# Where the second half of a shared expert's products runs: between the first experts, or ahead of them

## The chip, the cores and the metric

The kernel runs on one core of one Trainium2 chip. The metric is device time in microseconds (us) of one execution. The kernel before took 1657.83 us, the median of three runs from 1657.65 to 1658.01 us. All numbers of the inside of the kernel are from one further execution, which the hardware profiler recorded.

## The reference, cut to what matters

A decoder trunk with two layers over 272 tokens (16 learned ones and 256 of the input) of width 1024, all in float32. Each layer has a token mixer (RWKV-7 in layer 0, sliding-window attention in layer 1) and then a mixture of experts, which is where the change lies:

```
def swiglu(x, wg, wu, wd):
    return (jax.nn.silu(x @ wg) * (x @ wu)) @ wd

def moe_ffn(x2d, router, bias, w_gate, w_up, w_down, sh_gate, sh_up, sh_down):
    ...  # each token picks 8 of 64 experts; the tokens of an expert are gathered
    y = swiglu(x2d[tok], w_gate[e], w_up[e], w_down[e])     # for each expert
    ...
    return swiglu(x2d, sh_gate, sh_up, sh_down) + routed    # and one shared expert for all tokens
```

Each expert has a gate and an up matrix of 1024 x 256 and a down matrix of 256 x 1024: 1 MB each, 3 MB an expert, 192 MB a layer. The shared expert has the same shapes and is applied to all 272 tokens.

## The kernel before, in words

The program has one instruction stream for each engine. They meet at semaphores, and within one engine the order is that of the program.

**The stream of expert weights.** SyncE (SP) issues all expert weights, each as one transfer of 1 MB, in the order gate and up of expert e, then down of expert e-1 (`sp_experts`, which calls `sp_load`, issue in line 844). On chip there is room for four experts. So the first four experts' weights are fetched while the token mixer still runs. Gate and up of expert 4 may be issued only when the gate and up product of expert 0 is done (semaphore `L.gu`), and so on with a distance of four; a down matrix waits for the down product four experts earlier (`L.down`).

**One expert on TensorE** (`pe_expert`), in this order: the gate and up product (`mm_gate_up`, line 781, 16 matmuls, 32 passes in the trace, since each float32 matmul shows as two); the turning of the next expert's gathered token rows (`pe_turn_x`, line 769); the pick of the indices of the expert three ahead (`pe_pick`, line 762); the turning of this expert's gate and up results (line 788); and the down product of the expert before (`mm_down`, line 799). VectorE copies the turned rows out of PSUM before the next gate and up product can start (line 774).

**The gathers.** GpSimd fetches the token rows of an expert by an indirect transfer (line 818) when VectorE has turned the picked values into indices (`take_index`, lines 812 to 814), and writes scaled results back by another (line 823).

**The shared expert.** Its 256 hidden columns are done in two halves of 128, as each half's result fills a PSUM bank. `mm_shared` (line 1006) issues for each of the eight slices of the width one matmul of 128 x 128 weights with 272 token columns. The first half of gate and of up (`sg0`, `su0`) is issued during the routing, ahead of the experts. The second half (`sg1`, `su1`) uses the same two banks, so `sg1` may start when ScalarE has read `sg0` (semaphore step `sg0` of `moe_act`), and `su1` when VectorE has multiplied the first half (step `sm0` of `moe_dve`, line 1050). In the kernel before it stands between the experts: four matmuls of `sg1` after expert 0 and four after expert 1, four of `su1` after expert 2 and four after expert 3. ScalarE applies silu to `sg1` after its part of expert 2, and after its part of expert 4 it waits for `su1` and issues the load of the shared down matrix (1 MB, on its own queue).

**Ahead of the first expert** (`pe_experts`), TensorE issues one product without use, the picks for experts 0, 1 and 2, each of which waits for VectorE, then four products without use (`keep_busy`, line 998: 512 columns each, 8 passes in the trace; the result goes to a bank that is overwritten), and then turns the rows of expert 0.

`SETS` = 4 is the number of experts held, `E` = 64 the number of experts.

Of the kernel before, what the change touches and what calls it, by code (L numbers as in the profile page):

```python
# [35 lines left out]
KC = D // P  # L36
# [84 lines left out]
def hybrid_trunk(nc, I, out):  # L121
    with ExitStack() as ctx:
# [3 lines left out]
        def sem(name):  # L126
            return ctx.enter_context(nc.semaphore(name))
# [125 lines left out]
        def ln_steps(t, halves=True):  # L253
# [29 lines left out]
                  for l in range(2)]  # L283
        moe_act = [Steps(sem(f"route_act{l}"), [(f"hT{t}", 1) for t in H_ORDER[l]] + [("sig", 1), ("sc", 1), ("sg0", 1), ("sg1", 1)]) for l in range(2)]
        moe_dve = [Steps(sem(f"route_dve{l}"),
                         [(f"{n}{t}", 1) for n, t in zip(("hT", "row", "hT", "row", "row"), ROW_ORDER[l])]
                         + [("choice", 1), ("top2", 24), ("gs", 1), ("rank", 5), ("hide", 1), ("mask", 1),
                            ("top8", 3), ("taken", 3), ("sel", 1), ("g0", 1), ("gsum", 1), ("g1", 1), ("g2", 1),
                            ("kr", 1), ("dest", 3), ("posm", 1), ("max", 1), ("maxi", 1), ("sm0", 1), ("sm1", 1),
                            ("sd", 6)]) for l in range(2)]  # L290
# [425 lines left out]
        def num(e, times=1, add=0, per=1):  # L716

            i, k = e
            v = times * (k // per) + add
            return v if isinstance(i, int) else i * (UNROLL * times // per) + v  # L720

        def wait(eng, s, value):

            if not isinstance(value, int) or value > 0:
                eng.wait_ge(s, value)

        def early(e, k):

            return isinstance(e[0], int) and e[1] == k

        def plus(e, k):
            return (e[0], e[1] + k)
# [6 lines left out]
        def e_slots(e):  # L739

            s0 = 3 * (e[1] % SETS)
            return s0, s0 + 1, s0 + 2
# [34 lines left out]
        def mm_gate_up(dst, s):  # L777

            for k in range(KC):
                for j in range(2):  # L780
                    mm = nc.tensor.matmul(dst[SLOTS * j:SLOTS * j + SLOTS, 0:FF], xgT[:, k, :],  # L781
                                          slot_of(s + j)[:, FF * k:FF * k + FF], start=(k == 0), stop=(k == KC - 1))
            return mm

        def mm_turn(dst):

            for j in range(2):
                mm = nc.tensor.transpose(dst[:, P * j:P * j + P], guc[:, P * j:P * j + P], ident[:, :])  # L788
            return mm
# [5 lines left out]
        def mm_down(dst, s, hid):  # L795

            for j in range(2):
                for half in range(2):
                    mm = nc.tensor.matmul(dst[SLOTS * half:SLOTS * half + SLOTS, :], hid[:, j, :],  # L799
                                          slot_of(s)[:, D * j + 512 * half:D * j + 512 * half + 512],  # L800
                                          start=(j == 0), stop=(j == 1))
            return mm
# [43 lines left out]
        def pe_pick(pe, L, e):  # L846

            pe.wait_ge(L.onehot, num(e, 1, L.base + 1))
            wait(pe, L.index, num(e, 1, L.base))
            mm_pick(ps[:, bV, :], hot[e[1] % 2], column(values, e, 3)).then_inc(L.values, 1)  # L850

        def pe_turn_x(pe, L, l, e):
            pe.wait_ge(L.gathered[e[1] % 4], num(e, 16, 4 * L.base + 16, per=4))
            wait(pe, L.xt_copied, num(e, 1, L.base))
            mm_turn_x(ps[:, bU, :], xs[e[1] % 4]).then_inc(L.xt, 1)

        def pe_expert(pe, L, l, e, this=True):
            after, three_after, prev = ahead(e, 1), ahead(e, 3), e_before(e)
            if this:
                s0, s1, _ = e_slots(e)  # L860
                pe.wait_ge(L.xt_copied, num(e, 1, L.base + 1))
                pe.wait_ge(slot_loaded[s0], num(e, 16, L.slot_base[s0] + 16, per=SETS))
                pe.wait_ge(slot_loaded[s1], num(e, 16, L.slot_base[s1] + 16, per=SETS))
                wait(pe, L.gu_copied, num(e, 1, L.base))
                mm_gate_up(ps[:, bG, :], s0).then_inc(L.gu, 1)
            if this and after:
                pe_turn_x(pe, L, l, plus(e, 1))
            if this and three_after:
                pe_pick(pe, L, plus(e, 3))
            if this:  # L870
                copied, hidden = num(e, 1, L.base + 1), num(e, 1, L.base)
                if not isinstance(copied, int):
                    pe.reg_add(copied_count, copied_count, 1)
                    pe.reg_add(hidden_count, hidden_count, 1)
                    copied, hidden = copied_count, hidden_count
                pe.wait_ge(*moe_dve[l].at("choice"))
                pe.wait_ge(L.gu_copied, copied)
                wait(pe, L.hid, hidden)
                mm_turn(ps[:, bR, :]).then_inc(L.turned, 1)
            if prev:  # L880
                q = plus(e, -1)
                s2 = e_slots(q)[2]
                pe.wait_ge(L.hid, num(q, 1, L.base + 1))
                if early(q, 0):
                    pe.wait_ge(*moe_dve[l].at("maxi"))
                pe.wait_ge(slot_loaded[s2], num(q, 16, L.slot_base[s2] + 16, per=SETS))
                wait(pe, L.y_a, num(q, 1, L.base - 1))
                wait(pe, L.y_v, num(q, 1, L.base - 1))
                mm_down(ps[:, bY[q[1] % 2], :], s2, hidT[q[1] % 2]).then_inc(L.down, 1)
# [78 lines left out]
        def over_experts(eng, body):  # L968

            for k in range(HEAD):  # L970
                body((0, k))
            with eng.Fori(0, (E - HEAD - TAIL) // UNROLL) as i:
                for j in range(UNROLL):
                    body((i, HEAD + j))
            for k in range(E - TAIL, E):
                body((0, k))

        def ahead(e, k):

            return not isinstance(e[0], int) or e[1] + k < E  # L980

        def e_before(e):
            return not isinstance(e[0], int) or e[1] >= 1
# [9 lines left out]
        SPARE_BANK = (7, 2)  # L993

        def keep_busy(bank, n):

            for _ in range(n):
                nc.tensor.matmul(ps[:, bank, :], ident[:, :], headrow[:, 0:512], start=True, stop=True)  # L998

        def mm_shared(pe, l, name, ks):  # L1000

            which, half = name[1], int(name[2])
            j = "gu".index(which)
            for k in ks:
                w = shared_w[j][:, FF * k:FF * k + FF].rearrange("p (m j) -> p j m", j=2)
                m = nc.tensor.matmul(ps[:, bS[j], 0:T], w[:, half, :], mhT[:, k, :], start=(k == 0), stop=(k == KC - 1))  # L1006
                if k == KC - 1:
                    m.then_inc(*moe_pe[l].step(name))

        def pe_experts(pe, L, l):  # L1010
            pe.reg_mov(copied_count, num((0, HEAD - 1), 1, L.base + 1))
            pe.reg_mov(hidden_count, num((0, HEAD - 1), 1, L.base))
            keep_busy(SPARE_BANK[1], 1)
            pe_pick(pe, L, (0, 0))
            pe_pick(pe, L, (0, 1))
            pe_pick(pe, L, (0, 2))
            keep_busy(SPARE_BANK[1], 4)
            pe_turn_x(pe, L, l, (0, 0))

            def body(e):  # L1020
                pe_expert(pe, L, l, e)
                if early(e, 0):
                    pe.wait_ge(*moe_act[l].at("sg0"))
                if early(e, 2):
                    pe.wait_ge(*moe_dve[l].at("sm0"))
                if isinstance(e[0], int) and e[1] < 4:
                    mm_shared(pe, l, ("sg1", "su1")[e[1] // 2], range(KC // 2 * (e[1] % 2), KC // 2 * (e[1] % 2) + KC // 2))
            over_experts(pe, body)
            pe_expert(pe, L, l, (0, E), this=False)

        def act_silu(act, l, half):
# [357 lines left out]
        def _(pe):  # L1389
# [373 lines left out]
            def moe(l, prev_dve):  # L1763
# [36 lines left out]
                m.then_inc(*st.step("pos"))  # L1800
                set_main(l)
                pe_experts(pe, main, l)
                pe.wait_ge(*moe_dve[l].at("sm1"))
                pe.wait_ge(shared_loaded[2], 16 * (l + 1))
# [1002 lines left out]
```

## Time and profile before

| what | value |
|---|---|
| runs, median (lowest to highest) | 1657.83 us (1657.65 to 1658.01) |
| span of the profiled execution, first to last instruction | 1659.9 us, 33659 instructions |
| mean granted TensorE clock | 0.968 |
| TensorE busy | 1469.7 us (89%) |
| VectorE, ScalarE, GpSimd busy | 619.0, 318.7, 331.5 us |
| DMA moved | 508.21 MB, mean 306 GB/s; 456.49 MB of it on SP's queue |

The profile states no time of the profiled execution but its span, which is 2.07 us (0.12%) above the median of the runs. Times inside the trace count from the first instruction. The experts of layer 0 run from about 388 to 902 us, those of layer 1 from about 1102 to 1617 us. PE is TensorE's matmuls, SPq the issue of transfers by SP, DVE VectorE, ACT ScalarE, POOL GpSimd. "PEclk" is the granted TensorE clock as a share of its upper level, 2.4 GHz, so that 0.50 is the lower level, 1.2 GHz. "DMA share" is the mean busy share of the 16 DMA engines; it can read a little over 1.

### The profile page before, as it was taken

How to read it: one execution, taken by the hardware profiler on the slowest of the kernel's cores; microseconds unless marked ns; L12 is line 12 of the kernel's file. 1: busy time of each engine (PE TensorE's matmuls, PEld its weight loads, DVE VectorE, ACT ScalarE, POOL GpSimd, SP SyncE). 2: the span in 40 equal slices, each digit the busy share in tenths (PEclk: the TensorE clock that was granted, in tenths of full speed). 3: DMA queues.
4: the chain of work that ended last, by engine and by line, in shares of the span. 5: the costliest groups of instructions: out<-in, count | busy, mean ns of one | idle time of the engine just before them, and what ended most of it. 6: DMA issues, size and time to landing. Idle time of an engine off the chain costs nothing.

```text
span 1659.9 us, 33659 instructions
## 1 busy us (share of the span) xinstructions
PE 1469.7 (89%) x12824; PEld 952.7 (57%) x12824; DVE 619.0 (37%) x1580; ACT 318.7 (19%) x743; POOL 331.5 (20%) x412
## 2 busy tenths in 40 slices
PE   6989988899998888888888698999998888888886
PEld 4776877656665555555554267466655555555542
DVE  5362352673333333333332704543333333333327
ACT  1521332110111111111111015111111111111110
POOL 6012000021222222222221210122222222222210
PEclk9999988899999999999999799999999999999998
DMA  6330002349999999999997961299999999999986
GB/s 198 124 113 1 4 4 80 105 175 370 403 414 415 416 415 415 415 416 415 415 416 312 366 184 52 94 376 396 414 415 416 416 415 415 416 415 416 416 339 246
DMA packets 139862, 508.21 MB, mean 306 GB/s; under 512 B 29273, under 2 KB 58273, under 8 KB 104188
## 3 DMA queue, kind: packets, MB, share of 16 engines
q1 hardware_dynamic: 103312, 456.49, 68.9%
q0 software_dynamic: 22288, 41.89, 7.0%
q10 hardware_dynamic: 14172, 8.54, 1.8%
q8 instruction: 67, 1.10, 0.3%
q14 instruction: 23, 0.19, 0.0%
HBM read 501.38 MB, written 36.90 MB: 324 GB/s over the span
## 4 chain that ended last, share of the span: by engine, by line
PE 44%; SPq 23%; DMA 22%; DVE 6%; issue 3%; ACT 1%; ACTq 0%; DVEq 0%; POOL 0%; POOLq 0%
SPq L844 23%; DMA arena<-in_moe_w_up 21%; PE ps L781 9%; PE ps L1423 6%; PE ps L799 3%; PE ps L1553 3%; PE ps L1006 2%; PE ps L1865 2%; PE ps L1967 2%; PE ps L762 1%; PE ps L769 1%; PE ps L1748 1%; DMA arena<-routed 1%; PE ps L1849 1%; PE ps L998 1%
## 5 line engine op out<-in xcount | busy, mean ns | idle before, releaser
L781 PE MATMUL ps<-arena 128*64 128x256 f32 x2048 | 234.5, 381 | 57.2 <-DMA arena<-in_moe_w_up 57.2
L781 PE MATMUL ps<-ring,arena 128*64 128x256 f32 x2048 | 234.6, 381 | 51.8 <-DMA ring<-in_moe_w_up 38.5
L774 DVE COPY arena<-ps 128x512 f32<-128x512 f32 x128 | 88.6, 692 | 514.1 <-PE ps L769 514.1
L781 PEld LDWEIGHTS ps<-arena 128*64 128x64 f32 x2048 | 163.4, 137 | 151.5 <-issue 106.4
L818 POOL DMA_INDIRECT arena<-hrows,arena x128 | 129.7, 1013 | 586.0 <-DVE arena L814 572.0
L781 PEld LDWEIGHTS ps<-ring,arena 128*64 128x64 f32 x2048 | 154.5, 137 | 154.0 <-issue 79.0
L823 POOL DMA_INDIRECT routed<-arena x128 | 118.2, 924 | 240.2 <-DVE arena L942 175.8
L942 DVE TENSOR_SCALAR arena<-ps,arena 64x512 f32<-64x512 f32 x128 | 95.1, 743 | 162.1 <-PE ps L799 162.1
L896 ACT COPY arena<-ps 128x256 f32<-128x256 f32 x128 | 47.6, 372 | 537.0 <-PE ps L781 537.0
L906 ACT ACTIVATE arena<-ps,arena 64x512 f32<-64x512 f32 x128 | 87.5, 683 | 206.1 <-PE ps L799 206.1
L799 PE MATMUL ps<-ring,arena 128*64 128x512 f32 x512 | 124.0, 605 | 0.0
L799 PE MATMUL ps<-arena 128*64 128x512 f32 x512 | 123.5, 604 | 0.0
L762 PEld LDWEIGHTS ps<-arena 128*128 128x128 f32 (+1 forms) x768 | 105.6, 190 | 6.1 <-issue 2.3
L762 PE MATMUL ps<-arena 128*128 (+2 forms) x768 | 105.8, 242 | 2.1 <-DVE arena L814 1.6
L769 PE MATMUL ps<-ident,arena 128*128 128x128 f32 x512 | 83.8, 286 | 0.0
L769 PEld LDWEIGHTS ps<-ident,arena 128*128 128x128 f32 x512 | 53.7, 140 | 49.7 <-issue 49.7
L1423 PE MATMUL ps<-arena,ring 128*128 128x272 f32 x256 | 63.9, 415 | 8.8 <-DVE arena L2342 4.4
L806 DVE SCALAR_TENSOR_TENSOR arena<-arena 128x384 f32<-128x384 f32 x128 | 69.1, 541 | 0.1
L900 ACT ACTIVATE arena<-ps 128x128 f32<-128x128 f32 x128 | 35.5, 277 | 152.4 <-PE ps L788 152.4
L1423 PEld LDWEIGHTS ps<-arena,ring 128*128 128x128 f32 x256 | 51.7, 203 | 20.8 <-DVE arena L2292 4.8
L799 PEld LDWEIGHTS ps<-arena 128*64 128x64 f32 x512 | 31.2, 136 | 48.1 <-issue 48.1
L799 PEld LDWEIGHTS ps<-ring,arena 128*64 128x64 f32 x512 | 31.0, 136 | 47.3 <-issue 47.3
(375 smaller groups left out, 1595.4 us busy)
## 6 DMA issues: line engine op xcount, KB each, us to landing
ring<-in_moe_w_gate SPq DMA_DIRECT2D x64, 1024.0 KB
ring<-in_moe_w_up SPq DMA_DIRECT2D x64, 1024.0 KB
ring<-in_moe_w_down SPq DMA_DIRECT2D x64, 1024.0 KB
arena<-in_moe_w_gate SPq DMA_DIRECT2D x64, 1024.0 KB
arena<-in_moe_w_up SPq DMA_DIRECT2D x64, 1024.0 KB
arena<-in_moe_w_down SPq DMA_DIRECT2D x64, 1024.0 KB
arena<-routed SPq DMA_DIRECT2D x16, 1024.0 KB, 14.3
ring<-in_attn_w_qkv SPq DMA_DIRECT2D x6, 1024.0 KB
```

Of the source, the lines that this page charges most:

```text
L762: mm = nc.tensor.matmul(dst[:, 0:3], hot[0:n, t, :], vals[0:n, t, :], start=(t == 0), stop=(t == NT - 1))
L769: mm = nc.tensor.transpose(dst[:, P * j:P * j + P], rows[:, P * j:P * j + P], ident[:, :])
L774: return nc.vector.tensor_copy(xgT.rearrange("p (r j) m -> p j r m", r=2), ps[:, bU, :].rearrange("p (j r m) -> p j r m", j=4, r=2))
L781: mm = nc.tensor.matmul(dst[SLOTS * j:SLOTS * j + SLOTS, 0:FF], xgT[:, k, :], slot_of(s + j)[:, FF * k:FF * k + FF], start=(k == 0), stop= ...
L799: mm = nc.tensor.matmul(dst[SLOTS * half:SLOTS * half + SLOTS, :], hid[:, j, :], slot_of(s)[:, D * j + 512 * half:D * j + 512 * half + 512 ...
L806: return nc.vector.scalar_tensor_tensor(out=hot, in0=iota_s[:, order, :].unsqueeze(1).to_broadcast([P, NT, 2 * SLOTS]), scalar=float(first ...
L818: return nc.gpsimd.indirect_dma_start(out=dst, out_offset=None, in_=hrows_d[l], in_offset=bass.IndirectOffsetOnAxis(ap=index, axis=0), bou ...
L823: return nc.gpsimd.indirect_dma_start(out=routed[l], out_offset=bass.IndirectOffsetOnAxis(ap=index, axis=0), in_=src, in_offset=None, boun ...
L844: sp.dma_start(slot_view(s), src).then_inc(slot_loaded[s], 16)
L906: nc.scalar.activation(ysc[q[1] % 4][:, 512:1024], ps[SLOTS:P, bY[q[1] % 2], :], ACT.Copy, scale=gate_s[q[1] % 8][SLOTS:P]).then_inc(L.y_a, 1)
L942: nc.vector.tensor_scalar(ysc[q[1] % 4][:, 0:512], ps[0:SLOTS, bY[q[1] % 2], :], gate_s[q[1] % 8][0:SLOTS], None, ALU.mult).then_inc(L.y_v, 1)
L1423: m = mm_(b[:, 0:T], slot3(s)[:, k, P * (c % 2):P * (c % 2) + P], xm[MIXBUF[mix]][:, k, :], start=(k == 0), stop=(k == KC - 1))
```

## The change

The four products without use that stand between the picks and the turning of expert 0's rows are taken out. In their place stands the whole second half of the shared expert's gate and up products, 16 matmuls (32 passes) of 272 columns, with the two waits on `sg0` and `sm0`. The four pieces between experts 0 to 3 are gone, so that each expert runs straight after the one before. The other engines' streams are as they were.

```
             pe_pick(pe, L, (0, 2))
-            keep_busy(SPARE_BANK[1], 4)
+            pe.wait_ge(*moe_act[l].at("sg0"))
+            mm_shared(pe, l, "sg1", range(KC))
+            pe.wait_ge(*moe_dve[l].at("sm0"))
+            mm_shared(pe, l, "su1", range(KC))
             pe_turn_x(pe, L, l, (0, 0))
-
-            def body(e):
-                pe_expert(pe, L, l, e)
-                if early(e, 0):
-                    pe.wait_ge(*moe_act[l].at("sg0"))
-                if early(e, 2):
-                    pe.wait_ge(*moe_dve[l].at("sm0"))
-                if isinstance(e[0], int) and e[1] < 4:
-                    mm_shared(pe, l, ("sg1", "su1")[e[1] // 2], range(KC // 2 * (e[1] % 2), KC // 2 * (e[1] % 2) + KC // 2))
-            over_experts(pe, body)
+            over_experts(pe, lambda e: pe_expert(pe, L, l, e))
             pe_expert(pe, L, l, (0, E), this=False)
```

The function that both versions call:

```
        def mm_shared(pe, l, name, ks):
            which, half = name[1], int(name[2])
            j = "gu".index(which)
            for k in ks:
                w = shared_w[j][:, FF * k:FF * k + FF].rearrange("p (m j) -> p j m", j=2)
                m = nc.tensor.matmul(ps[:, bS[j], 0:T], w[:, half, :], mhT[:, k, :], start=(k == 0), stop=(k == KC - 1))
                if k == KC - 1:
                    m.then_inc(*moe_pe[l].step(name))
```

## Rows read from the trace of the kernel before

**Rows 1.** The page: TensorE's busy time, and the DMA share in 40 slices.

```profile
PE 1469.7 (89%) x12824; PEld 952.7 (57%) x12824; DVE 619.0 (37%) x1580; ACT 318.7 (19%) x743; POOL 331.5 (20%) x412
...
DMA  6330002349999999999997961299999999999986
```

**Rows 2.** The chain that ended last, in order of time (start, us, what).

```profile
497.28 25.20 DMA arena<-in_moe_w_up
```

**Rows 3.** Stages: window, busy us per engine (instructions), PEclk, DMA share, GB/s.

```profile
500.00:600.00 100.00, 87.62 (x648) 54.59 (x644) 30.59 (x86) 16.08 (x37) 24.13 (x25) 1.00 1.02 415
...
1214.00:1314.00 100.00, 87.08 (x640) 53.94 (x638) 30.50 (x86) 16.00 (x37) 24.10 (x25) 1.00 1.02 415
```

**Rows 4.** Stages of two us about the end of expert 0's product, layer 0.

```profile
390.00:392.00 2.00, 2.00 (x22) 1.17 (x18) 0.00 (x0) 0.00 (x0) 0.00 (x0) 1.00 0.07 29
392.00:394.00 2.00, 2.00 (x16) 1.80 (x15) 0.99 (x4) 0.52 (x2) 0.00 (x0) 1.00 0.52 70
```

**Rows 5.** Timeline of SP: gate loads of experts 4 and 5 in layer 0.

```profile
392.25 0.33 SPq L844 DMA_DIRECT2D ring<-in_moe_w_gate  x1
...
399.46 0.35 SPq L844 DMA_DIRECT2D ring<-in_moe_w_gate  x1
```

**Rows 6.** Timeline of TensorE: start, us, line, operands, count.

```profile
26.57 10.77 PE L1423 MATMUL ps<-arena,ring 128*128 128x272 f32 x35 [4.35 <-DVE arena L2292]
...
366.40 6.69 PE L1006 MATMUL ps<-arena 128*128 128x272 f32 x28
...
380.68 6.63 PE L998 MATMUL ps<-headrow,ident 128*128 128x512 f32 x8
387.15 0.60 PE L769 MATMUL ps<-ident,arena 128*128 128x128 f32 x4
...
393.65 2.01 PE L1006 MATMUL ps<-arena 128*128 128x272 f32 x8
...
402.66 2.11 PE L1006 MATMUL ps<-arena 128*128 128x272 f32 x8
...
1095.13 6.10 PE L998 MATMUL ps<-headrow,ident 128*128 128x512 f32 x8
1101.07 0.60 PE L769 MATMUL ps<-ident,arena 128*128 128x128 f32 x4
```

**Rows 7.** Stages: the granted clock ahead of the first expert, layers 0 and 1.

```profile
379.80:386.60 6.80, 6.80 (x12) 3.36 (x12) 0.99 (x6) 0.00 (x0) 2.31 (x3) 0.50 1.02 417
...
1093.20:1100.00 6.80, 6.30 (x12) 3.61 (x13) 1.33 (x9) 0.00 (x0) 3.05 (x3) 0.50 1.03 421
```

**Rows 8.** Stages of line 1423 alone: PE, PEld, then PEclk, DMA share, GB/s.

```profile
31.00:31.60 0.60, 0.60 (x3) 0.48 (x2) 0.50 0.36 143
31.60:33.00 1.40, 1.40 (x7) 1.13 (x7) 0.99 0.01 3
```

**Rows 9.** Line 1006: duration of one pass (ns, min/median/max), first and last start.

```profile
L1006 PE MATMUL ps<-arena x128: 392/392/506, 365.0 to 1136.5; 128*128 128x272 f32 x128
```

**Rows 10.** Line 1050 on VectorE (end of the first half), and the gathers' landing.

```profile
381.37 0.44 DVE L1050 TENSOR_TENSOR arena<-arena,ps 128x272 f32<-128x272 f32 x1
...
DMA to landing us min/median/max: 6.2/6.7/7.7
```

**Rows 11.** Stages of ten us after the restart of the weight stream, layers 0 and 1.

```profile
400.00:410.00 10.00, 10.00 (x68) 6.27 (x69) 3.37 (x11) 1.34 (x3) 1.95 (x2) 1.00 1.01 383
410.00:420.00 10.00, 10.00 (x66) 5.90 (x68) 2.78 (x8) 2.01 (x5) 1.98 (x3) 1.00 1.01 395
420.00:430.00 10.00, 10.00 (x68) 5.90 (x66) 2.49 (x7) 1.34 (x3) 2.81 (x3) 1.00 1.01 388
...
1114.00:1124.00 10.00, 10.00 (x67) 6.27 (x69) 3.29 (x11) 1.40 (x4) 1.95 (x2) 1.00 1.04 417
1124.00:1134.00 10.00, 10.00 (x66) 5.90 (x66) 2.78 (x8) 1.95 (x5) 2.08 (x3) 1.00 0.99 372
1134.00:1144.00 10.00, 10.00 (x68) 5.88 (x65) 2.49 (x7) 1.34 (x3) 2.82 (x3) 1.00 0.99 380
```

## The prediction

> **What bounds the kernel now.** I read the page first, then the chain in order of time, then the experts' stage in windows. The page says TensorE is busy 89% of the span, but its DMA line stands at 9 in two long stretches [rows 1]; these are the experts of the two layers, and they need windows of their own. There the chain is a trap. It follows TensorE through the experts to 497 us and only there steps over to a weight transfer [rows 2], as if TensorE set the time until then. But a chain that follows a transfer goes back to its issue, and does not see that the transfer stood in a queue: this one took 25.20 us for 1 MB, while the windows show 415 GB/s, at which 1.05e6 bytes need 2.5 us. So some ten transfers stood ahead of it. The windows settle it: over a hundred us of each layer the DMA share is 1.02 at 415 GB/s, while TensorE is busy 87 of 100 us [rows 3]. The weight stream is the bound of this stage, and it ends a fixed time after its last idle moment: bytes left over rate. What counts for the change is therefore when the stream is not at its full rate.
>
> There are two such places. First, before expert 4's weights. The four sets on chip are full at about 390 us; SP may go on when expert 0's gate and up product is done, and issues at 392.25 [rows 5]. In between the stream falls to 29 and then 70 GB/s [rows 4]. Second, after that restart. For 30 us it runs at 383, 395 and 388 GB/s in layer 0 and at 417, 372 and 380 in layer 1, in place of 415 [rows 11]. Here TensorE frees sets hardly faster than they are fetched: an expert with a piece of the shared product is 9.1 us (from 393.65 to 402.66, piece to piece [rows 6]), and 3.15 MB of weights at 415 GB/s are 7.6 us, without the gathers. The queue runs nearly dry before each issue.
>
> **The change, part by part.** *The stretch ahead of expert 0.* Before, 8 passes without use start at 380.68 and the turning of expert 0's rows at 387.15; in layer 1 at 1095.13 and 1101.07 [rows 6]. The clock stands at 0.50, its lower level of 1.2 GHz, from 379.8 to 386.6 and from 1093.2 to 1100.0 [rows 7], after the short picks that wait for VectorE. In place come 32 passes of 272 columns. At the upper level one costs 0.233 us: 28 take 6.69 us, less 0.39 for the last one's duration, over 27 steps [rows 6, 9]. At the lower level I take twice that, 0.467 us. That can be tested on line 1423, which has the same shape and begins at the lower level: it starts at 26.57, the clock rises at 31.6 [rows 8], so 5.03 / 0.467 = 10.8 passes, and the remaining 10.77 - 0.39 - 5.03 = 5.35 us hold 22.9 more; with the last one 34.7 against 35 counted [rows 6]. The same rows show that a stream of this shape is followed by a rise of the clock as the products without use are.
>
> With the rise where it is now, layer 0 does (386.6 - 380.68) / 0.467 = 12.7 passes slowly and 19.3 x 0.233 = 4.5 us of the rest, to 391.1; the turning starts 3.95 us later than 387.15. Layer 1: (1100.0 - 1095.13) / 0.467 = 10.4, then 21.6 x 0.233 = 5.0, to 1105.0, which is 3.95 us later than 1101.07. Both layers: **+7.9 us**. Nothing hides this: the rows' gather, the weights of expert 0 and VectorE's copy are done or follow the turning as they do now. Expert 0's product, and with it SP's issue at 392.25, moves by the whole of it, and the stream is idle in that time.
>
> *The waits.* `sg0` is read by ScalarE during the routing. `sm0` comes from line 1050, which ends at 381.8 [rows 10]; `su1` is reached after 16 slow passes at the earliest, 380.68 + 16 x 0.467 = 388.1. Behind the wait would stand the turning and all experts, but it is met 6.3 us early, so its cost is 0, and 0 again in layer 1, where VectorE's order is the same. The bounds of a wait that passes at once are 0 and one pass, 0.5 us in both layers together; I take 0.
>
> *The pieces between experts.* Eight passes leave each of experts 0 to 3: 2.01 us of the first, 2.11 of a later one [rows 6], 8.3 us by these rows, 32 x 0.233 = 7.5 by the passes. TensorE then reaches expert 4 about 4 us earlier in each layer, in spite of the start. But TensorE is not the bound, so this is worth only what the stream was slowed by: the shortfall from 415 GB/s. Over ten us each it is 0.77, 0.48 and 0.65 us in layer 0 and -0.05, 1.04 and 0.84 in layer 1, as 10 x (415 - rate) / 415 [rows 11]; together 3.7 us. How much comes back no row shows, so it lies between 0 and 3.7; a gain over 3.7 would need a rate above 415, which no long window has. I take the last two of each three, **-3.0 us**: the first stretch still has only the 3 MB that expert 0's product releases, and the next set follows when expert 1's product is done (7.2 us later now, 399.46 [rows 5], about 5.3 then). After that sets come free every 7.0 us (9.1 less a piece of 2.1), quicker than the 7.6 us of a fetch, so the queue fills.
>
> The Trainium skill, page "DMA: Bandwidth & Descriptors", section "Rules for kernel authors", says that a transfer's fixed setup cost overlaps when it is issued early. By that rule a deeper queue would hide all of the shortfall, and the sum would be 7.9 - 3.7 = +4.2 us; the trace agrees so far as the full rate stands where the queue is deep, but no run here shows the queue deepened at this place.
>
> *What else moves.* The picks inside the experts, and the gathers that POOL issues from them, come 3.95 us later for expert 3 and then relatively earlier. A gather lands within 6.2 to 7.7 us [rows 10] and is needed two experts after its pick, some 14 us after without the pieces; a gather that is late would cost TensorE a few tenths, and the queue covers that. The load of the shared down matrix on ScalarE's queue waits for `su1`, which is done long before; it stays behind ScalarE's part of expert 4, with the same 1 MB. VectorE's and ScalarE's instructions are unchanged and wait for less.
>
> **Sum:** 7.9 - 3.0 = +4.9 us on the span of 1659.9 us, so 1664.8. The runs shown have a median 2.07 us below that span; the same difference on it gives 1657.83 + 4.9 = **1662.7 us**, +0.3%. What this measurement can tell from no change is about 0.2%, 3.3 us.
>
> **The rivals.**
>
> *Nothing of the shortfall comes back* (the dips are the gathers' or the memory's doing, not the queue's): +7.9, 1665.7 us. For it: the DMA share is already 0.99 to 1.04 in the slow stretches [rows 11]. Against it: gathers run all through the stage, and later it holds 415.
>
> *TensorE is the bound up to 497 us after all*, as the chain has it [rows 2]. Then the pieces' 8 us less the start's 3.95 count in full, 4.05 a layer, and the time is 1657.83 - 8.1 = 1649.7 us, faster. It would need spare DMA between 394 and 497, of which rows 11 show less than 2 us a layer. Chance small.
>
> *The clock rises late.* If the shared passes did not bring the clock up before they end, 32 x 0.467 = 14.9 us would end at 395.6 and 1110.0, 8.5 and 9.0 us later than now; with -3.0 that is +14.5, 1672.3 us. Line 1423 speaks against it [rows 8].
>
> *More comes back than the shortfall in those stretches*, because the stream's rate from 394 on is raised a little everywhere: at +3 or below this reads as no change, about 1660. Or the idle time at the start proves shorter than the shift, with the same result: the four sets would have to be full later than 390, which row 390 to 392 speaks against [rows 4].
>
> **How the numbers follow.** The forecast's own case, from all of the shortfall back to most of it lost (+3.8 to +6.5): 0.60. Nothing back: 0.14. Late clock: 0.03. Little or no net change: 0.14. TensorE the bound: 0.09. Slower by over 0.2% takes the first three, 0.77, less 0.02 for a forecast that falls just below the line: 0.75; within 0.2%: 0.16; faster: 0.09. The range leaves out the fast case, the late clock and a little of the third and reaches from 1660.2 to 1666.0, from +2.4 to just over the case with nothing back.
>
> **What would show it.** In the profile after: the turning of expert 0 at about 391.1 and 1105.0, with 32 passes of line 1006 ahead of it and the clock at 0.50 until about 386.6 and 1100.0; SP's first issue at about 396.2; an idle stretch of the stream from 390 to about 397; the ten us windows from 406 on at 410 to 416 GB/s; experts 0 to 3 at 7 us each. The prediction is wrong if the first issue comes less than 3 us later, if the stream shows gaps after it as before, or if the last product of layer 0 comes earlier than now although the first issue came later.

## The result, and the profile after

The changed kernel takes 1663.85 us, the median of 20 runs (1657.60 to 1675.65), against 1657.92 us for the kernel before (20 runs, 1652.50 to 1670.36): a ratio of 1.0038, 95% interval 1.0022 to 1.0055. Timed once more beside before (e7 below) it is 1.0021, 1.0001 to 1.0041. So it is slower, by some 0.2 to 0.4%; 1662.7 us was forecast.

The profiled execution seems to say the opposite: its span is 1656.8 us, shorter than the 1659.9 us of before. It was one of the shorter executions of the changed kernel (1658.51 us, fourth lowest of the 20). The page, to be held against [rows 1]:

```profile
span 1656.8 us, 33627 instructions
...
PE 1455.1 (88%) x12808; PEld 951.3 (57%) x12808; DVE 618.3 (37%) x1580; ACT 318.7 (19%) x743; POOL 330.3 (20%) x412
...
DMA  6420002358999999999998961389999999999986
```

The contradiction is solved by counting each layer's experts from their own beginning. TensorE's timeline of the changed kernel (start, us, line, operands, count): the first pick of each layer, in layer 0 the second pick with the idle time ahead of it, the 32 passes, the turning, and the gate and up product of expert 63.

```profile
371.77 0.92 PE L762 MATMUL ps<-arena 128*128 128x3 f32 x6
373.21 0.89 PE L762 MATMUL ps<-arena 128*128 128x3 f32 x6 [0.53 <-DVE arena L814]
...
375.83 10.49 PE L1006 MATMUL ps<-arena 128*128 128x272 f32 x32
386.15 0.60 PE L769 MATMUL ps<-ident,arena 128*128 128x128 f32 x4
...
891.18 3.67 PE L781 MATMUL ps<-arena 128*64 128x256 f32 x32 [1.37 <-DMA arena<-in_moe_w_up]
...
1086.28 0.92 PE L762 MATMUL ps<-arena 128*128 128x3 f32 x6
...
1090.76 9.72 PE L1006 MATMUL ps<-arena 128*128 128x272 f32 x32
1100.32 0.60 PE L769 MATMUL ps<-ident,arena 128*128 128x128 f32 x4
...
1605.39 3.68 PE L781 MATMUL ps<-arena 128*64 128x256 f32 x32 [1.33 <-DMA arena<-in_moe_w_up]
```

SP's timeline of the changed kernel, which answers to [rows 5]: the gate loads of experts 4 and 5 in layer 0, and of expert 4 in layer 1.

```profile
391.25 0.33 SPq L844 DMA_DIRECT2D ring<-in_moe_w_gate  x1
...
396.62 0.35 SPq L844 DMA_DIRECT2D ring<-in_moe_w_gate  x1
...
1105.42 0.33 SPq L844 DMA_DIRECT2D ring<-in_moe_w_gate  x1
```

And the rows of the kernel before that are needed for the same count: first pick and last gate and up product of each layer on TensorE,

```profile
376.65 0.92 PE L762 MATMUL ps<-arena 128*128 128x3 f32 x6
...
894.38 3.67 PE L781 MATMUL ps<-arena 128*64 128x256 f32 x32 [1.36 <-DMA arena<-in_moe_w_up]
...
1090.84 0.92 PE L762 MATMUL ps<-arena 128*128 128x3 f32 x6
...
1608.58 3.67 PE L781 MATMUL ps<-arena 128*64 128x256 f32 x32 [1.39 <-DMA arena<-in_moe_w_up]
```

and SP's first issue in layer 1 (the one in layer 0 is in [rows 5]):

```profile
1106.17 0.33 SPq L844 DMA_DIRECT2D ring<-in_moe_w_gate  x1
```

The differences of these starts, with those of the experiments' profiles, worked out in the same way (us; "start" is from the first pick to the first issue for expert 4, "stream" from there to the start of expert 63's product; layer 0 / layer 1):

| kernel | start | stream | both together |
|---|---|---|---|
| before | 15.60 / 15.33 | 502.13 / 502.41 | 517.73 / 517.74 |
| before, second profile (e8) | 15.59 / 15.29 | 502.12 / 502.00 | 517.71 / 517.29 |
| changed | 19.48 / 19.14 | 499.93 / 499.97 | 519.41 / 519.11 |
| changed, second profile (e7) | 19.34 / 19.08 | 500.22 / 500.12 | 519.56 / 519.20 |
| e1 pieces left out | 15.20 / 15.38 | 500.23 / 500.03 | 515.43 / 515.41 |
| e2 start later still | 22.91 / 22.54 | 500.23 / 499.98 | 523.14 / 522.52 |
| e3 shared down load early | 19.48 / 19.30 | 497.76 / 497.62 | 517.24 / 516.92 |
| e4 begun between the picks | 15.07 / 15.07 | 500.15 / 499.97 | 515.22 / 515.04 |
| e5 = e4 and e3 | 15.07 / 15.07 | 497.65 / 498.17 | 512.72 / 513.24 |
| e6 half of it ahead | 15.56 / 15.48 | 500.14 / 500.39 | 515.70 / 515.87 |

The change makes the start 3.88 and 3.81 us later and the stream 2.20 and 2.44 us shorter: +1.68 and +1.37, together +3.05 us. With the two second profiles it is +1.85 and +1.91, +3.76 us. The stages of one kernel repeat within 0.5 us. What hides them in a single span is the time before the first pick, which is 4.9 us shorter in this profile of the changed kernel, and the time between the layers, 1.4 us shorter; e7 and e8 tell of both.

The chain reads as before ([rows 2]): TensorE first, then a transfer that took 25 us because it queued.

```profile
494.02 25.14 DMA arena<-in_moe_w_up
```

The windows of the changed kernel (busy us per engine, PEclk, DMA share, GB/s) answer to [rows 7], [rows 4], [rows 11] and [rows 3], in that order:

```profile
374.90:381.60 6.70, 6.70 (x18) 5.27 (x18) 0.99 (x6) 0.00 (x0) 2.33 (x3) 0.50 1.03 421
...
388.00:390.00 2.00, 2.00 (x22) 1.33 (x20) 0.00 (x0) 0.00 (x0) 0.00 (x0) 1.00 0.00 0
390.00:392.00 2.00, 2.00 (x20) 1.40 (x16) 0.16 (x1) 0.37 (x1) 0.00 (x0) 1.00 0.00 0
392.00:394.00 2.00, 2.00 (x18) 1.44 (x19) 1.59 (x6) 0.28 (x1) 0.34 (x1) 1.00 0.86 242
394.00:400.00 6.00, 6.00 (x48) 3.56 (x46) 1.33 (x6) 0.70 (x3) 1.79 (x2) 1.00 1.00 414
400.00:410.00 10.00, 10.00 (x84) 6.16 (x80) 3.65 (x9) 2.36 (x5) 2.90 (x3) 1.00 1.02 413
410.00:420.00 10.00, 10.00 (x74) 6.09 (x72) 3.77 (x12) 1.98 (x5) 2.25 (x3) 1.00 1.03 417
...
500.00:600.00 100.00, 86.73 (x631) 53.64 (x632) 30.32 (x86) 16.27 (x37) 23.20 (x25) 1.00 1.02 415
```

Here one sees both sides of the change: four whole us at 0 GB/s while TensorE is at work, and then the full rate from the first window on, where layer 0 of before had 383 to 395. The six us ahead of [rows 11], in the kernel before:

```profile
394.00:400.00 6.00, 6.00 (x48) 4.08 (x46) 0.87 (x3) 0.50 (x2) 1.14 (x1) 1.00 0.97 399
```

### The profile page after: what moved, and what is told of

Its sections match the earlier page's. It is cut to its first block, busy times and chain, and to the rows that moved or that the text cites. A ratio compares the mean times of both kernels' runs of the same rounds, so it can differ in the third digit from the quotient of the medians.

```text
span 1656.8 us, 33627 instructions
## 1 busy us (share of the span) xinstructions
PE 1455.1 (88%) x12808; PEld 951.3 (57%) x12808; DVE 618.3 (37%) x1580; ACT 318.7 (19%) x743; POOL 330.3 (20%) x412
## 4 chain that ended last, share of the span: by engine, by line
PE 41%; SPq 27%; DMA 23%; DVE 6%; issue 3%; ACT 1%; DVEq 0%; POOL 0%; POOLq 0%
SPq L844 27%; DMA arena<-in_moe_w_up 21%; PE ps L781 8%; PE ps L1417 6%; PE ps L1547 3%; PE ps L799 2%; PE ps L1006 2%; PE ps L1859 2%; PE ps L1961 2%; PE ps L762 1%; DMA arena<-routed 1%; PE ps L1742 1%; PE ps L1843 1%; PE ps L1754 1%; PE ps L769 1%
```

## The experiments

e1 and e6 are shown as edits of the kernel before, e2 to e5 as edits of the changed kernel. `...` stands for lines and arguments not shown.

**e1: the pieces left out.**

```
                 if early(e, 0):
                     pe.wait_ge(*moe_act[l].at("sg0"))
+                    mm_shared(pe, l, "sg1", [KC - 1])
                 if early(e, 2):
                     pe.wait_ge(*moe_dve[l].at("sm0"))
-                if isinstance(e[0], int) and e[1] < 4:
-                    mm_shared(...)
+                    mm_shared(pe, l, "su1", [KC - 1])
```

The kernel leaves out seven of the eight matmuls of each product, `sg1` and `su1`. The last one stays, so that the semaphore steps come as they did; a further edit in `mm_shared` lets it start its sum by itself.

> The kernel before, with the second half's gate and up products cut to one matmul of eight each (leaves out seven eighths of them), in the places where they stood: the pieces between experts all but gone, the start of expert 0 as before. Theory (the weight stream is the bound, and the pieces cost it only the shortfall after its restart): first issue for expert 4 at 15.5 us after the first pick as before, from there to the last gate and up product 499.9 us a layer in place of 502.1 to 502.4, in all about -4.6 us against before. Rival A (the dips after the restart are the gathers' or the memory's doing): 502 us, no gain. Rival B (TensorE is the bound up to expert 19): 8 us less a layer less two passes, about -15 us.

1653.77 us (12 runs) against 1658.81 (35 runs), ratio 0.9962, 0.9942 to 0.9982. The start is as before and the stream 500.1 us: 1.9 and 2.4 us less. The windows of e1, in the stretch of [rows 11], show where from:

```profile
400.00:410.00 10.00, 10.00 (x78) 5.94 (x76) 3.65 (x9) 2.37 (x5) 2.89 (x3) 1.00 1.03 420
410.00:420.00 10.00, 10.00 (x78) 6.22 (x74) 3.50 (x12) 1.98 (x5) 1.92 (x2) 1.00 1.02 412
420.00:430.00 10.00, 10.00 (x78) 5.79 (x76) 4.31 (x11) 2.02 (x4) 2.94 (x3) 1.00 1.02 415
```

The gathers are the same and the dips are gone, so the dips were not the gathers' doing. Nor is TensorE the bound: 28 passes fewer a layer, 6.5 us, are worth 2.3 us by both stages together.

**e2: the start later still.**

```
             pe_pick(pe, L, (0, 2))
+            keep_busy(SPARE_BANK[1], 4)
             pe.wait_ge(*moe_act[l].at("sg0"))
```

> The changed kernel with the four products without use put back ahead of the second half's products, so that expert 0 starts later still. Theory (each us of a later start of expert 0 is a us of an idle weight stream, one to one): the products without use take the low clock, the 32 passes then run at 0.233 us, so that the first issue is about 3.5 us later than in the changed kernel, 23 us after the first pick, from issue to last product 499.9 us as there: about +7 us against the changed kernel in both layers, +10 against before. Rival (the start is covered by the sets on chip, and only the experts' own pace counts): as the changed kernel.

1669.15 us (12 runs), ratio to before 1.0066, 1.0042 to 1.0090. TensorE's timeline of e2:

```profile
390.91 6.46 PE L998 MATMUL ps<-headrow,ident 128*128 128x512 f32 x8
397.21 7.50 PE L1006 MATMUL ps<-arena 128*128 128x272 f32 x32
404.55 0.60 PE L769 MATMUL ps<-ident,arena 128*128 128x128 f32 x4
```

At the upper level the 32 passes take 7.34 us from first start to the turning. The start is 3.4 us longer than the changed kernel's, the stream the same 500.1, so 3.7 and 3.4 us a layer go through to the end, one to one. The sets on chip cover none of it.

**e3: fill the idle stretch.** The load of the shared down matrix is moved on ScalarE's queue from behind expert 4 to the front.

```
         def act_experts(act, L, l):
+            act.wait_ge(*moe_pe[l].at("su1"))
+            act.dma_start(shared_w[2], I["shared_w_down"][l]...).then_inc(shared_loaded[2], 16)
             def body(e):
...
-                if early(e, 4):
-                    act.wait_ge(*moe_pe[l].at("su1"))
-                    act.dma_start(shared_w[2], I["shared_w_down"][l]...)
```

> The changed kernel with the load of the shared down matrix (1 MB, ScalarE's queue) issued as soon as su1 is done, ahead of expert 0, in place of after expert 4: it falls into the stretch in which the weight stream is idle. Theory (the stream's idle time is what the change costs): 1 MB at 415 GB/s is 2.5 us a layer that is no longer taken from the stream later, so issue to last product 497.4 us in place of 499.9, about -5 us against the changed kernel and about -2 us against before by the stages. Rival (that load is hidden anyway, on a queue of its own): as the changed kernel.

1657.57 us (12 runs), ratio to before 0.9984, 0.9964 to 1.0004: by the runs no difference from before can be told. By the stages the stream is 497.7 us, 2.2 and 2.4 us less than the changed kernel's, for 2.5 expected. The windows of e3 show the load in the gap (its end in layer 0; SP's issue follows at 396.13):

```profile
392.00:394.00 2.00, 1.59 (x16) 1.09 (x18) 0.82 (x2) 0.00 (x0) 0.00 (x0) 1.00 0.89 246
394.00:396.00 2.00, 2.00 (x20) 1.12 (x16) 0.00 (x0) 0.00 (x0) 0.00 (x0) 1.00 0.66 279
396.00:398.00 2.00, 2.00 (x18) 1.72 (x18) 0.99 (x4) 0.64 (x2) 0.00 (x0) 1.00 0.48 70
```

The same megabyte costs 2.2 to 2.4 us behind expert 4 and next to nothing here: a load on another queue isn't hidden where the stream is the bound.

**e4: begin between the picks.**

```
+            pe.wait_ge(*moe_act[l].at("sg0"))
             pe_pick(pe, L, (0, 0))
+            mm_shared(pe, l, "sg1", range(0, 2))
             pe_pick(pe, L, (0, 1))
+            mm_shared(pe, l, "sg1", range(2, 4))
             pe_pick(pe, L, (0, 2))
-            pe.wait_ge(*moe_act[l].at("sg0"))
-            mm_shared(pe, l, "sg1", range(KC))
+            mm_shared(pe, l, "sg1", range(4, KC))
```

> The changed kernel with the second half's products begun earlier: two matmuls of sg1 after the first pick, two after the second, the rest after the third. Theory (the start is late because 32 passes follow the picks and some of them run at the lower clock): the gaps in which TensorE waits for VectorE are filled, and if the clock then stays at its upper level, 32 passes are done at about 387 us of the profile of before, so that the first issue stands at about 15.6 to 16.5 us after the first pick, and issue to last product at 499.9: about -2.3 to -1.3 us a layer against before, -3 to -4.5 in all. Rival (the clock falls all the same): the first issue at 18 to 19.5 us after the first pick, time as the changed kernel or up to 2 us below it.

1652.52 us (12 runs), ratio to before 0.9971, 0.9948 to 0.9993. TensorE's timeline and a window of e4:

```profile
374.05 0.89 PE L762 MATMUL ps<-arena 128*128 128x3 f32 x6
374.87 1.19 PE L1006 MATMUL ps<-arena 128*128 128x272 f32 x4
375.90 0.81 PE L762 MATMUL ps<-arena 128*128 128x3 f32 x6
376.64 1.19 PE L1006 MATMUL ps<-arena 128*128 128x272 f32 x4
377.67 0.81 PE L762 MATMUL ps<-arena 128*128 128x3 f32 x6
378.41 5.78 PE L1006 MATMUL ps<-arena 128*128 128x272 f32 x24
384.02 0.60 PE L769 MATMUL ps<-ident,arena 128*128 128x128 f32 x4
```

```profile
374.00:379.90 5.90, 5.85 (x33) 5.31 (x33) 2.51 (x14) 0.00 (x0) 2.43 (x3) 1.00 1.03 426
```

Eight passes stand in the gaps in which the picks waited for VectorE, and the clock stays at 1.00 through the stretch in which it fell before ([rows 7]). All 32 useful passes then end 9.97 us after the first pick; the 8 without use of before ended after 10.50 and 10.23. The first issue, 15.07 us after the first pick, comes sooner than the 15.6 to 16.5 us that I expected. The wait on `sg0`, which now stands ahead of the first pick, hides nothing from this count: the first pick starts 1.20 us after the product without use ahead of it in e4, 1.12 us in before. So the start costs nothing, and the stream's 2.0 and 2.4 us remain as gain.

**e5: e4 and e3 together.** Both edits, as shown.

> The second half's products begun between the picks, as in e4, and the load of the shared down matrix issued as soon as su1 is done, as in e3. Theory (start of expert 0 and idle time of the weight stream add up): first issue for expert 4 at 15.1 us after the first pick, issue to last product 497.6 us, first pick to last product 512.7 us in each layer, 5 us below before in each, about -10 us in all. Rival (the load, which now runs while the first four sets are still being fetched, only pushes their end back and delays expert 0 or the gathers): the first issue later than 15.5 or issue to last product at 500, time as e4.

1648.27 us (6 runs) against 1659.33 (23 runs), ratio 0.9931, 0.9909 to 0.9953, the fastest of all. Start as e4, stream 497.65 and 498.17 for 497.6 expected; together 5.0 and 4.5 us a layer below before. The stream's windows about the first issue (389.13 in layer 0) have a gap of some 0.9 us left, worked out from their rates against 415 GB/s; the 29 and 70 GB/s of [rows 4] make 3.5 us:

```profile
386.00:388.00 2.00, 2.00 (x22) 1.34 (x20) 0.00 (x0) 0.00 (x0) 0.00 (x0) 1.00 1.05 424
388.00:390.00 2.00, 2.00 (x21) 1.40 (x15) 0.28 (x1) 0.37 (x1) 0.00 (x0) 1.00 0.86 354
390.00:392.00 2.00, 2.00 (x19) 1.38 (x20) 1.47 (x6) 0.28 (x1) 0.46 (x1) 1.00 0.98 283
```

**e6: half of the change.**

```
-            keep_busy(SPARE_BANK[1], 4)
+            pe.wait_ge(*moe_act[l].at("sg0"))
+            mm_shared(pe, l, "sg1", range(KC))
             pe_turn_x(pe, L, l, (0, 0))
...
-                if early(e, 0):
-                    pe.wait_ge(*moe_act[l].at("sg0"))
...
-                if isinstance(e[0], int) and e[1] < 4:
-                    mm_shared(...)
+                if early(e, 2) or early(e, 3):
+                    mm_shared(pe, l, "su1", ...)      # the two halves of su1, as before
```

> Half of the change: sg1 ahead of expert 0 in place of the products without use, su1 in two pieces after experts 2 and 3 as before. Theory (the price is the passes that the start takes longer, 16 of 272 columns against 8 of 512): at the lower level 12 to 13 of the 16 passes cover the time of the products without use, so that the first issue stands at 15.4 to 16.0 us after the first pick (before 15.3 to 15.6); issue to last product between 500.0 and 501.3 us, since the two pieces that are left slow the stream once more; about -1 to -3 us in all against before. Rival (any piece ahead delays the start by as much as it saves later): time as before or above it.

1655.39 us (12 runs) against 1659.33, ratio 0.9988, 0.9966 to 1.0010: inconclusive by the runs, -2.0 and -1.9 us by the stages. The start is that of before. The surprise is the stream: 500.14 and 500.39, the full gain, although two pieces still stand behind experts 2 and 3. The windows of e6 (the pieces begin at 402.51 and 411.63) show no dip at them:

```profile
396.00:406.00 10.00, 10.00 (x72) 6.19 (x70) 3.40 (x9) 2.12 (x5) 2.89 (x3) 1.00 1.02 417
406.00:416.00 10.00, 10.00 (x72) 6.18 (x70) 2.48 (x7) 1.34 (x3) 1.93 (x2) 1.00 1.03 415
```

SP's timeline of e6: the gate loads of experts 4, 5 and 6 in layer 0.

```profile
387.01 0.33 SPq L844 DMA_DIRECT2D ring<-in_moe_w_gate  x1
...
392.38 0.35 SPq L844 DMA_DIRECT2D ring<-in_moe_w_gate  x1
...
399.30 0.33 SPq L844 DMA_DIRECT2D arena<-in_moe_w_gate  x1
```

So taking away the first two pieces was enough: without them SP's second set comes 5.37 us after the first (7.2 before, [rows 5]; 5.37 in the changed kernel too, by its rows of SP) and the third 12.3 us after it (16.3 before, where it was issued at 408.56), and the rate holds. Which of the two pieces counts for more, e6 does not tell.

**e7 and e8: both kernels once more.** No edit.

> The changed kernel once more, for the place of the difference between its stages (first pick to last gate and up product +1.7 and +1.4 us against before, +3.1 in all) and its medians (+6.3 us). Theory (the difference is in the stages of the experts; the token mixers, whose instructions are the same, take a different time in each execution as their clock steps fall): the stages repeat within 0.5 us, the time before the first pick differs by several us between profiles, and the ratio comes out between 1.001 and 1.004. Rival (the change makes some other part longer by 3 us): the stages between the experts or after them are longer than in before, again and by the same amount.

> The kernel before once more, for one more profile. Theory: first pick to last product 517.7 us in both layers within 0.5, while the time before the first pick of layer 0 (376.65 in the first profile) and between the layers (196.46) differ by some us from the first profile. Rival: these repeat as the experts' stages do, so that the changed kernel's 371.77 before the first pick is the change's doing.

The changed kernel: 1662.06 us (12 runs) against 1659.33, ratio 1.0021, 1.0001 to 1.0041; before: one run of 1655.98. The stages are in the table. The time before the first pick of layer 0 was 376.65 and 371.55 us in the two profiles of before, 371.77 and 376.37 in the two of the changed kernel: the same two values on either side, so it isn't the change's doing. A window in the token mixer, for before, changed, changed again (e7) and before again (e8), shows a part of it:

```profile
58.00:72.00 14.00, 14.00 (x75) 8.01 (x77) 11.41 (x24) 6.65 (x13) 0.53 (x1) 0.76 0.32 96
```

```profile
58.00:72.00 14.00, 14.00 (x119) 9.41 (x119) 12.41 (x28) 10.35 (x19) 0.53 (x1) 1.00 0.50 151
```

```profile
58.00:72.00 14.00, 14.00 (x105) 8.36 (x104) 12.03 (x26) 7.33 (x14) 0.53 (x1) 0.76 0.36 105
```

```profile
58.00:72.00 14.00, 14.00 (x120) 9.39 (x117) 12.81 (x29) 10.47 (x20) 0.53 (x1) 1.00 0.53 164
```

In the two executions with 376 us the clock is lower here, and VectorE and ScalarE, which live on TensorE's results, got less done in the same 14 us (11.41 and 12.03 against 12.41 and 12.81; 6.65 and 7.33 against 10.35 and 10.47). At a mean of 0.76 the window should cost 14 x 0.24 = 3.4 us of the 5, an estimate. Counted in VectorE's instructions it is 3.3: from the one that starts at 58.68 us in the changed kernel to the one at 83.85, it takes 25.17 us there and 25.19 in e8, but 28.50 in before and 28.51 in e7. The rest comes later in the mixer and was not traced.

The rival, a longer part between or behind the experts, did not show. From expert 63's product to the first pick of layer 1 it was 196.46 and 196.31 us before, 195.10 and 194.68 with the change: shorter, not longer. That it repeats so well for each kernel is not what I expected of e8. The other six profiles lie between 194.53 (e6) and 197.08 (e1), and e3, which has the changed kernel's TensorE program, took 196.66; so I take it for scatter, but it isn't explained. Behind expert 63's product in layer 1 it was 51.3 to 51.4 us in all four. From the first pick of layer 0 to the end of the span, all told, the change costs 1.8 and 2.2 us in the two pairs.

## Why the prediction was right, point by point

- **The bound.** Right. e2 puts a later start through to the end one to one, e3 gains 2.2 to 2.4 us by moving 1 MB into the idle stretch, and e1 gets 2.3 us for 6.5 us less of TensorE's work. The chain's reading, TensorE up to 497 us, would have made the change faster by 8 us.
- **The start.** Forecast 3.95 us a layer, measured 3.88 and 3.81 (3.75 and 3.79 in the second pair). The clock fell and rose as said: at the lower level for 6.7 us, and up again under the 272 column passes as under the products without use.
- **The waits** cost nothing: the 32 passes stand in the trace as one block, with no idle time ahead of the second half.
- **The pieces.** This is the term that was mis-sized. I took 3.0 us of a shortfall of 3.7, and 4.6 us came back (2.20 + 2.44; 3.8 in the second pair). That the first pair gives more than 3.7 is in part scatter, up to 0.4 us a layer in the stream, and in part a stretch that my windows left out: from 394 to 400 the kernel before stood at 399 GB/s, another 0.2 us. I kept the first ten us of the shortfall because "the first stretch still has only the 3 MB that expert 0's product releases". In its place the runs show 414 and 413 GB/s from the first window on, and e6 shows how little it takes: without the first two pieces the second release comes 1.8 us sooner and the third 4.0 us, and the rate holds. The weight was in those two pieces, which I had given nothing in the first stretch. I also read the pace of the pieces the wrong way round: a set freed every 9.1 us is not "hardly faster" than a fetch of 7.6 us but slower, 346 GB/s without the gathers, so the queue had to run dry.

  The Trainium skill, page "DMA: Bandwidth & Descriptors", section "Rules for kernel authors", says that the fixed setup cost of a DMA overlaps when it is issued early and waited for late. As the prediction used it, by that rule all of the shortfall was to come back, and the trace agrees as to the amount: 4.6 and 3.8 us of 3.7. No run here shows that what came back was setup cost; a queue that runs empty would look the same.
- **The sum.** +4.9 us forecast; +3.05 and +3.76 by the two pairs of profiles; +0.38% (0.22 to 0.55) and +0.21% (0.01 to 0.41) by the two sets of runs, that is 6.3 and 3.5 us. The forecast lies among these. That the first median, 1663.85, came within 1.2 us of the forecast is in part luck: the start was sized right, the stream's gain was put too low, and the medians differ by some 2 to 3 us more than the stages that the change touches. That the first set of runs gave more than the stages is not explained by any part of the trace; the intervals overlap from 0.22 to 0.41%, 3.6 to 6.8 us, and the stages lie at or just below the lower end of that. Whether the change is worth a little more or a little less than 0.2% stays open.
- **What the prediction got wrong in its own tests.** I gave absolute times (turning at 391.1, first issue at 396.2). They came at 386.15 and 391.25, since the mixer ended 4.9 us sooner in that execution, and by the test "first issue less than 3 us later" the prediction would have failed. Counted from the first pick the issue is 3.88 us later. A test by times of one execution must name the row that it counts from.

## What to carry to other kernels

Where a stream of loads is the bound, ask of each edit only two things: does it move the release that restarts the stream, and does the stream run dry after it. Ahead of the release each us cost a us here (e2); behind it, work of the compute engine cost only what it starved the stream of, 2.3 us for 6.5 (e1), and nothing that could be told once the stream was ahead (e6). Useful work in place of products without use is a gain only as far as it takes no longer; put into the gaps between waiting instructions (e4) it took no more time here than those products, and a load in the stream's idle stretch (e3, e5) took next to none. When executions differ by more than the change, compare stages counted from a row of their own.

## What the runs showed of the hardware that was not expected

The clock falls in a stretch in which TensorE seems busy: ahead of expert 0 the idle gaps between the picks are some 0.5 us each, and the clock is at 0.50 behind them; in e4, with eight passes put into them, it stays at 1.00. And one and the same kernel, before, reached its first pick at 371.55 us in one profile and at 376.65 in the other: 5 us, more than what this change is worth, of which 3.3 fall in the stretch where the clock's mean was 0.76 in place of 1.00.
